# Row scale of the norms applied to products as they leave PSUM, unscaled tiles split during the projection ahead, adaLN shift as two more columns

## Reference

```
first block, layer 0:  x += pool_attn_mixer(rms_norm(x, g0));  x += conv_ffn(rms_norm(x, g1))
first block, layer 1:  x += rglru_mixer(rms_norm(x, g2));      x += conv_ffn(rms_norm(x, g3))
second block:          h = rms_norm(x, g4) * (1 + sc1) + sh1;  p = h @ w_in
                       x += gt1 * (sum over 4 branches of sigmoid(p gate) * y_branch) @ w_o
                       h = rms_norm(x, g5) * (1 + sc2) + sh2
                       x += gt2 * (relu(h @ w1)**2 @ w2)
                       return rms_norm(x, g6)
rms_norm(x, g) = x * rsqrt(mean(x*x over channels) + 1e-6) * g
conv_ffn(h)    = (gelu(conv3(h @ w_in)_g) * conv3(h @ w_in)_u) @ w_out
```

## Time and profile before

| what | us |
|---|---|
| median of 3 runs | 1231.25 (1230.45 to 1235.73) |
| profiled execution, its own time | 1227.34 |
| its span, first to last instruction | 1225.5 |
| PE busy | 1104.7 (90%) |
| DVE busy | 863.9 (70%) |
| ACT busy | 627.7 (51%) |
| POOL busy | 40.6 (3%) |

### The profile page before, as it was taken

How to read it: one execution, slowest core, us unless ns; L and a number is a source line. 1 busy time by engine, 2 the same in 40 slices (tenths; PEclk the granted TensorE clock), 3 DMA queues, 4 the chain that set the end, 5 groups by cost and what they waited for, 6 DMA issues and landing times.

```text
span 1225.5 us, 20826 instructions
## 1 busy us (share of the span) xinstructions
PE 1104.7 (90%) x8548; PEld 1042.7 (85%) x8548; DVE 863.9 (70%) x1442; ACT 627.7 (51%) x1056; POOL 40.6 (3%) x44
## 2 busy tenths in 40 slices
PE   4997799999968869799999988899999988999996
PEld 3974799999957658799999977789989977999996
DVE  6875788888976687787785464998885576555443
ACT  6444566665544685555564456322224446776441
POOL 0000200000001000000000100000000001000010
PEclk9999899999979899899999988999999988999998
DMA  8436555555542763365666643122333363556650
GB/s 296 128 108 237 188 172 187 184 172 172 195 149 100 244 212 118 119 243 200 246 233 223 214 131 107 44 86 87 106 132 105 120 214 120 191 184 196 185 159 35
DMA packets 59567, 200.40 MB, mean 164 GB/s; under 512 B 6608, under 2 KB 11344, under 8 KB 59216
## 3 DMA queue, kind: packets, MB, share of 16 engines
q1 hardware_dynamic: 57888, 194.54, 48.3%
q10 hardware_dynamic: 1584, 4.53, 1.1%
HBM read 197.99 MB, written 1.05 MB: 162 GB/s over the span
## 4 chain that ended last, share of the span: by engine, by line
PE 71%; DVE 18%; ACT 6%; issue 2%; DMA 2%; SPq 0%; DVEq 0%; ACTq 0%
PE ps L425 71%; DVE wlo L1446 4%; DMA ring<-rg_w_in 1%; ACT whi L955 1%; DVE rq L1629 1%; ACT L955 1%; DVE rst L1475 1%; DVE xr L1452 1%; ACT L L955 1%; DVE raw L1446 1%; DVE sc L1801 1%; DVE w L1446 1%; DVE xr L1811 0%; DVE raw L1452 0%; DVE cosT L1446 0%
## 5 line engine op out<-in xcount | busy, mean ns | idle before, releaser
L425 PE MATMUL ps<-hh,whi 128*128 128x256 f32 x1656 | 490.1, 296 | 49.4 <-DVE hl L1446 30.8
L425 PE MATMUL ps<-hl,whi 128*128 128x256 f32 x1656 | 478.6, 289 | 0.0
L425 PE MATMUL ps<-hh,wlo 128*128 128x256 f32 x1656 | 478.3, 289 | 0.0
L1446 DVE TENSOR_TENSOR wlo<-ring,whi 128x1024 fp32r<-128x1024 f32 (+1 forms) x313 | 375.1, 1211 | 72.5 <-ACT whi L955 71.7
L425 PEld LDWEIGHTS ps<-hh,whi 128*128 128x128 f32 x1656 | 328.1, 198 | 71.8 <-issue 42.9
L955 ACT ACTIVATE whi<-ring 128x1024 fp32r<-128x1024 f32 (+1 forms) x313 | 321.5, 1039 | 105.1 <-PE ps L425 62.6
L425 PEld LDWEIGHTS ps<-hl,whi 128*128 128x128 f32 x1656 | 328.6, 198 | 1.4 <-issue 1.0
L425 PEld LDWEIGHTS ps<-hh,wlo 128*128 128x128 f32 x1656 | 327.9, 198 | 0.0
L425 PE MATMUL ps<-hidh,whi 128*128 128x256 f32 x608 | 170.3, 280 | 0.0
L425 PE MATMUL ps<-hidl,whi 128*128 128x256 f32 x608 | 170.1, 280 | 0.0
L425 PE MATMUL ps<-hidh,wlo 128*128 128x256 f32 x608 | 170.1, 280 | 0.0
(11 more groups left out here) (318 smaller groups left out, 1336.2 us busy)
## 6 DMA issues: line engine op xcount, KB each, us to landing
ring<-ffn_w_in SPq DMA_DIRECT2D x88, 512.0 KB, 3.9
ring<-ffn_w SPq DMA_DIRECT2D x64, 512.0 KB, 4.1
ring<-w_in SPq DMA_DIRECT2D x51, 512.0 KB, 3.7
ring<-ada_w SPq DMA_DIRECT2D x48, 512.0 KB, 5.5
ring<-ffn_w_out SPq DMA_DIRECT2D x32, 448.0 KB, 4.5
ring<-rg_w_in SPq DMA_DIRECT2D x20, 512.0 KB, 4.6
ring<-pa_w_in SPq DMA_DIRECT2D x16, 512.0 KB, 5.2
ring<-ffn_w_out SPq DMA_DIRECT2D x16, 512.0 KB, 4.0
```

Source lines behind the costliest of these rows:

```text
L425: return e.matmul(o, l, r, start=start, stop=stop)
L1446: return e.tensor_tensor(o, a, b, op)
```

## The change

The tiles that a projection reads are no longer scaled by rst. `high_of_h` (ACT) and `low_of_h` (DVE) make hh and hl from x*g directly behind each tile's residual addition, and `h_tiles` is gone. `stats(n)` moves behind the first projection on PE (on ACT and DVE behind the `feed` for it), and every product is multiplied by rst as it leaves PSUM: `lift` on DVE for one tile, `lift_both` for two tiles that share a bank (`couple`). What ACT and DVE read from PSUM before, they read from SBUF now. For n > 3 the shift is put beside h as two more columns, so that these matmuls have 258 columns instead of 256; column 256 of the product is the shift's part, which `lift` copies into shw, and which is added later as a bias on ACT, or by a further DVE operation for w_in columns 0 to 6. In conv_ffn the work of two tiles goes together (gelu, product, split). In rglru tiles are projected in pairs. All squares are summed on POOL, and the output leaves in eight DMAs. vec is loaded first, by SP.

The pieces below are, in this order: the scalar program's `residual`; its and the vector program's operations; the tensor program of rglru; the vector program of conv_ffn; its columns of w_in; SP's output.

```
-ADA_IN = ((), (2, 5, 8, 11, 14, 17, 20))
-ADA_OUT = ((), (2,))
+ADA_IN = ((), (2, 5, 8, 11, 14, 17, 19, 21))
...
             def residual(n, w, nk, also=None):
...
                         gather(n, m)
                         if also:
                             also(m)
+                        if n < 6:
+                            high_of_h(n, m)
...
+            def high_of_h(n, m):
...
+                act(hh[:, m, 0:T], x[:, m, :], ACT.Copy, gain(n, m)).then_inc(*hhigh.up((n, m)))
...
+            def low_of_h(n, m):
...
+                stt(hl[:, m, 0:T], x[:, m, :], gain(n, m), hh[:, m, 0:T].bitcast(F32), MUL, SUB).then_inc(*hlow.up((n, m)))
+
+            def lift(o, w, m, nk=8):
+
+                if w in ("w_in", "ffn_w1"):
+                    through.wait_ge(e, tail(w, m, nk))
+                    e.tensor_copy(shw[:, m:m + 1], ps[where[w, m]][:, T:T + 1]).then_inc(*shifted.up((w, m)))
+                return tt(o, out_of(w, m, nk), rst[:, :], MUL)
+
+            def lift_both(o, w, m, m2):
+                through.wait_ge(e, tail(w, m2))
+                return tt(o, ps[where[w, m]][:, 0:2 * T].rearrange("p (c t) -> p c t", c=2), both(rst[:, :]), MUL)
...
-                project("rg_w_in", [10, 11, 12], 2)
-                for m in range(3):
-                    give(("rg_w_in", m + 10), rg_dve, ("x", m))
-                for m in range(3, 10):
-                    project("rg_w_in", [m + 10], 2)
-                    give(("rg_w_in", m + 10), rg_dve, ("x", m))
-                    if m == 3:
-                        ri(0)
-                        ri(1)
-                    ri(m - 1)
...
+                for m in range(0, 10, 2):
+                    couple("rg_w_in", m + 10, m + 11, 2)
+                    give(("rg_w_in", m + 10), rg_dve, ("lift", m))
+                    if m == 0:
+                        stats(2)
+                    else:
+                        ri(m - 2)
+                        ri(m - 1)
...
+                for m in range(25):
+                    if m < 22:
+                        feed(tail(w, m))
                         feed(tail(w, m + 22))
-                    taps(zg_, "g", m + 22, out_of(w, m + 22), m)
-                    behind(m)
+                        if m == 0:
+                            stats(2 * l + 1)
+                            mean.wait_ge(e)
+                        if m > 2:
+                            ff_dve.wait_ge(e, (l, "g", m - 3))
+                        lift_both(zl[l][:, m % 3, :, :], w, m, m + 22).then_inc(*ff_dve.up((l, "lift", m)))
+                    if 1 <= m < 23:
+                        taps(zu_, "u", m - 1, m - 1)
+                        taps(zg_, "g", m + 21, m - 1)
...
                     if m < 7:
                         o = lo_[:, :] if m == 6 else (fr, fk, fv)[m // 2][:, m % 2, :]
-                        p = out_of("w_in", m)
+                        lift(lifted[m], "w_in", m).then_inc(*rw_dve.up(("scaled", m)))
+                        rw_dve.wait_ge(e)
+                        shifted.wait_ge(e)
+                        ts(lifted[m], lifted[m], shift, None, ADD).then_inc(*rw_dve.up(("lift", m)))
+                        rw_dve.wait_ge(e)
                         rw_act.wait_ge(e, ("mix", m))
-                        stt(o[:, 1:], p[:, 0:T - 1], P("mu", m), o[:, 1:], MUL, ADD).then_inc(*rw_dve.up(("shift", m)))
+                        stt(o[:, 1:], lifted[m][:, 0:T - 1], P("mu", m), o[:, 1:], MUL, ADD).then_inc(*rw_dve.up(("shift", m)))
...
-            fin.wait_ge(e, 7)
-            e.dma_start(out, x[:, :, :]).then_inc(*x_out.up("all", 16))
+            for m in range(8):
+                fin.wait_ge(e, m)
+                e.dma_start(out[:, m, :], x[:, m, :]).then_inc(*x_out.up("all", 16))
```

More of the change, by code:

```diff
@@ L519, in head_norm @@
                     give(("hn", i), at_dve, ("hm", i))
[L520 to L526, removed]
+                for m in range(4, 12):
+                    single("pa_w_in", m, 0)
+                    give(("pa_w_in", m), at_dve, ("lift", m - 4))
+                    if m == 5:
+                        stats(0)
+                    if m > 6:
+                        head_norm(m - 7)
                 for m in range(12, 16):
[L528 to L531, removed]
+                    single("pa_w_in", m, 0)
+                    give(("pa_w_in", m), at_dve, ("v", m - 12))
+                    if m < 15:
+                        head_norm(m - 7)
                 def values():
@@ L1192, in ri @@
                     act(ii[:, m, :], ps[where["i", m]][:, 0:T], ACT.Sigmoid, bias=P("rg_bx", m)).then_inc(*rg_act.up(("i", m)))
-                feed(tail("rg_w_in", 12))
-                for m in range(3):
+                for m in range(2):
+                    rg_dve.wait_ge(e, ("lift", 0))
                     last_tap(m)
@@ L1246, in rglru @@
                             gather(3, m)
+                            high_of_h(3, m)
                     feed(number["rg_w_out", 0, k])
             def mixers():
+                feed(tail("w_in", 6))
+                stats(4)
                 stat.wait_ge(e, 4)
@@ L1897, in merge @@
                         tt(pm[:, m, :], pm[:, m, :], g, ADD).then_inc(*mx_dve.up(("sum", m, n)))
+                def merge(m, n):
+                    c = 19 + 8 * n + m
+                    feed(tail("w_in", c))
+                    if n == 0:
+                        s5_dve.wait_ge(e, ("turned back", m))
+                        lift(ga[:, m, :], "w_in", c).then_inc(*mx_dve.up(("lift", m, n)))
+                        product()
+                        return
+                    if before[m, n][0]:
+                        mx_dve.wait_ge(e, before[m, n][0])
+                    lift(gt[gslot[m, n][0]], "w_in", c).then_inc(*mx_dve.up(("lift", m, n)))
+                    feed(number["yw", m, YW[n][0]])
+                    product()
+                    late[0] = m, n
                 def sg():
```

572 lines of the change are left out of this document (286 added, 286 removed).

## The result

The changed kernel takes 1289.5 us (median of 4 runs, 1288.13 to 1290.80) against 1230.85: ratio 1.0469, 95% interval 1.0437 to 1.0500. It is 4.7% slower, where 1224 us and a range of 1203 to 1242 had been forecast. The profiled execution took 1288.6 us, 61.3 more than before's.

What follows compares the result with a forecast made beforehand. PE's work plus its idle stretches bound the kernel; five norms cost 54 us. Terms -6.7 - 4.8 - 7.5 + 1.5 + 8.3 + 1.0 + 1.9 - 0.7 = -7.0 gave 1220 us profiled, 1224 median; range 1203 to 1242.

Steps and rivals of the forecast that it cites:

- Norm 4 and w_in: Norm 4 through the branches: gain left 1.8 us, added DVE operations +3; net +1, bounds -10 and +18.
- Norm 5: Gap and restart of 8.5 us before ffn_w1 shrink to about 1 us: -7.5.
- The front: Start of kernel: PE begins some us earlier, but DVE paces the head norms: 0, bounds -3 and +4.
- norm 1: Gap and restart of 7.7 us before ffn_w_in0 shrink to about 1 us: -6.7.
- norm 4: Entry to w_in: first seven columns take DVE 2.9 to 3.04 us each; ACT's last column leaves a 1.8 us gain.
- norm 2 with rglru: Earlier start -9.2, chained pairs +10.2, last pair +2.3, gates +5: sum +8.3 us.
- ffn_w_out0: Stage before norm 2: later exit from ffn_w_in0 costs +1.5; DVE's adds 8.42 us apart against PE's 7.9.
- the gates: In rglru, five lifts of 0.60 us come onto a DVE busy 79%, with waits: +5.
- rival B: Norms' gaps gained, little given back in rglru and branches: -31, 1200 us; half of that, 1210; chance 0.27.
- norm 3: Before conv_ffn 1: 11.6 us of gap and restart become 6.8, POOL's squares and the reciprocal coming first: -4.8.
- The two more columns: 1992 matmuls in w_in and ffn_w1 get 258 columns instead of 256: +1.9 us.
- conv_ffn's pairs: DVE needs 5.3 us a pair, under PE's 5.7, so PE still bounds: 0.

Runs made afterwards that it cites:

- e4: Kernel before the change plus an unused 128x1 copy and 128x256 product on DVE, without waits, at each of w_in's 51 columns: 1225.3 us, ratio 0.9965.
- e11: Kernel before the change with added DVE copy and product at w_in's 51 columns, DVE waiting for PE's column ahead of them: 1238.0 us, ratio 1.0057.
- e8: Kernel before the change with only the product of a y tile made one merge later on DVE, nothing lifted: 1246.0 us, ratio 1.0132.
- e12: Kernel before the change with e11's added operations and wait, and e8's product one merge later: 1264.0 us, ratio 1.0271.
- e2: Changed kernel, but in ffn_w1 ACT makes hidh of the tile before ahead of its wait for the new lift: 1276.8 us, ratio 1.0387.
- e6: Changed kernel, but in rglru's first half DVE makes a pair's taps ahead of the next pair's lift: 1278.4 us, ratio 1.0396.
- e13: Kernel before the change with only an unused tile of 1028 bytes a partition, moving the tiles behind it: 1228.3 us, ratio 0.9959.
- e14: Kernel before the change with only an unused tile of 4 bytes a partition, moving the tiles behind it: 1223.3 us, ratio 0.9951.

## Why the prediction was wrong

**The step that failed** is the one in "Norm 4 and w_in": "In the branches 51 columns add 0.34 + 0.08 each to DVE; the idle in the busiest stretches is 3.7 and 4.4 us, which takes the first of them: +3", with its bound of +18. It counted what DVE has to do and left out when. The two counted prices were right (the lift paces at 0.33, the copy at 0.07), and e4 shows that they cost little by themselves (0.5 to 6.5 us). DVE's share in the branches, which was to rise above 95%, fell to 82% and 69%. From its tenth column on the stage lost 43.8 us, 37.5 of them by two waits that the sum has no term for: DVE waits for PE's column ahead of work that PE needs next (10.0 us, e11), and the multiplication that frees a y bank is made a merge later (18.0, e8), and the one makes the other worse (9.6, e12). The second can be read off the diff: before has the operation on pm in its own merge, the changed kernel in the next.

**ffn_w1** failed in the same manner. The prediction works out a DVE cycle against PE's for conv_ffn, and leaves ffn_w1 out. A loop of waits over ACT's order made 3.29 us out of it (e2). Norm 5 itself gave more than forecast: its gap went from 6.83 us to 0.13, and 26 products on, gap and restart had gained 8.5 us for the 7.5 forecast. The loop took 12.8 of it back: +4.3.

**The front** ("0, bounds -3 and +4") measured +7.4. The mechanism that it names, head norms paced by DVE, is what the trace shows: reciprocals stand 4.56 us apart instead of 4.22, one lift more. But the chain starts later, at 31.81 instead of 29.36, behind norm 0's own reciprocal and three lifts. The first and the eighth reciprocal, and the first scores behind them on PE (61.62 before):

```profile
31.81 1.76 DVE L1638 RECIPROCAL rq<-rq 128x256 f32<-128x256 f32 x1 [0.48 <-ACT rq L968]
63.71 1.75 DVE L1638 RECIPROCAL rq<-rq 128x256 f32<-128x256 f32 x1 [0.48 <-ACT rq L968]
66.13 1.61 PE L438 MATMUL ps<-qk 64*128 64x128 f32 x4 [9.43 <-DVE qk L1460]
```

PE's first product is 5.2 us earlier (13.7 for 18.9), which bought nothing, since it was DVE's chain that ended last. What the rest of the +7.4 is, behind the scores, was not looked into.

**Right in mechanism, near in size:** norm 1 (-7.4 for -6.7) and norm 4. For norm 2 with rglru (+11.4 for +9.8) the order is as forecast, DVE's taps behind the lift and PE's ri behind both, and e6 bears it out; but that the size is near is luck, since misses cancel. ffn_w_out0 lost 4.6 us: its first tile +1.4, for +1.5 forecast, and four later ones came at 8.4 us instead of 7.7, DVE's cycle of 8.42. `decay()` then ended 6.2 us earlier than in before (369.93 for 376.14), for 7.7 forecast. From there to the first gate product (415.70 for 403.53) 18.4 us were lost, for 12.5; the period of 11.9 us against 9.2 makes 8.1 of it for three pairs, and the rest wasn't looked into. From there to the end of rg_w_out it lost nothing (-0.8), where +5 had been forecast for the gates.

At norm 4 the columns come 3.06 us apart on DVE, for 2.9 to 3.04 forecast, and ACT's last operation on lo (now a part of raw) ends the gain, 756.06 where it was 744.70 in before:

```profile
733.65 0.48 DVE L1460 SCALAR_TENSOR_TENSOR kr<-rt,vec,kr 128x255 f32<-128x255 f32 x1 [0.65 <-ACT kr L968]
736.71 0.48 DVE L1460 SCALAR_TENSOR_TENSOR kr<-rt,vec,kr 128x255 f32<-128x255 f32 x1 [0.65 <-ACT kr L968]
756.06 0.41 ACT L968 ACTIVATE raw<-raw 64x256 f32<-64x256 f32 x1
```

**Slips in the working.** The terms listed for a column at norm 4 add up to 2.80, not 2.9 to 3.04; in the trace the lift takes 0.45 us before the add can start, and from the add to the tap 1.00 pass. In rglru a lift at +18, 0.7 for it and 6.8 of `decay()` end at +25.5, not +27.5. A pair has eight `ri` matmuls and not four; they took twice 1.10 us, and the 2.08 taken for them is four at a granted clock near 0.5, so the number came out near by luck. Half of rival B's gain is 1216 us, not 1210. The one in rglru is the largest in the sum, 2 us.

**Mis-sized:** norm 3, -4.8 forecast and +1.8 measured with conv_ffn 1. The gap gave 9.1 us, but the first pair took 11.6 us instead of 8.0, the pair behind each mod step some 0.5 more, and ffn_w_out1 65.5 instead of 63.6. The two more columns were put at +1.9 and cost nothing that shows: a column of ffn_w1 starts 2.88 us behind the last in e2 as in before, 0.120 us a product, where two columns in 256 would make 0.02 us a column. So here the columns alone don't set the pace. To this the Trainium skill has a rule (page "TensorE: Matmul & The Clock Gate", section "Back-to-back issue gap"): in a stream of weight loads and matmuls the spacing is set by both, in a pipeline. The trace agrees as far as it goes: it shows that the columns don't set the spacing by themselves, and not what the weight loads' part is. In conv_ffn's pairs DVE did stay under PE, as forecast: ffn_w_in0 has 1162 matmuls in 140 us where it had 1173, and the stage as a whole 127.1 us against 128.0.

## What to carry to other kernels

When an operation moves to an engine that executes in order, its price isn't its duration but what stands behind its wait: list for each such engine what is behind the new wait, and who is waiting for that, in every stage, the idle ones too. A multiplication or copy that empties a PSUM bank can be on PE's path, however cheap it is: putting one of 0.42 us off by one turn of the loop cost 15 us here. And a change that hides a gap is worth trying stage by stage: here norms 1, 3 and 5 alone come out 1.4% faster, and the whole 4.7% slower.

## What was not expected of the hardware

- 51 added operations of 0.42 us on DVE, in a stage in which DVE's durations fill over 90% of its busiest stretches, cost the stage 0.5 us against e13 and 6.5 against e14, and the kernel nothing that its median shows (e4).
- An unused tile of 4 bytes a partition sped up PE in ffn_w2 from 599 to 620 matmuls in 70 us at the same granted clock of 1.00 (e14), and one of 1028 bytes did the same (e13). That the remainder of the addresses matters and not the distance is a guess from these two; which tile's address it is, was not tried. In the changed kernel a shift to the same remainder helped ffn_w_out1 (65.5 to 63.0 us) and hardly ffn_w2 (92.8 to 92.1).
- The taps of conv_ffn, now read from SBUF, last as long as before from PSUM, 481 ns for 482. The group of the changed kernel's page:

```profile
L1460 DVE SCALAR_TENSOR_TENSOR zg<-zl,vec,zg 128x255 f32<-128x255 f32 x88 | 42.3, 481 | 1.6
```

- Matmuls of 258 columns came as fast as those of 256: from the first to the last of 24 in ffn_w1 2.74 to 2.78 us (e2) and 2.76 (before).
- pa_w_out took 32 us in most profiles and 27.6 (e4), 30 (e11, e12) or 29.3 (e6) in others, with the same instructions in that stage: single profiles differ by up to 4 us there.
